# Adding the squares of a norm on GpSimd: two rows for TensorE to sum instead of eight

## The chip, the cores and the metric

The kernel runs on one core of a Trainium2 chip. Its metric is the device time of one execution in microseconds (us), the median over runs. Five engines have their own instruction queues and meet through semaphores: TensorE (PE; its weight loads are listed apart as PEld), VectorE (DVE), ScalarE (ACT), GpSimd (POOL) and SyncE (SP), which issues most of the DMAs.

## The reference, cut to what matters

One inference step of a small hybrid decoder: 512 prompt tokens and 8 sample tokens, so N = 520 columns, with D_MODEL = 1024. Layer 0 mixes with a gated linear recurrence (HGRN2), layer 1 with sparse attention (NSA) over a key/value side that is projected once between the layers. Each layer adds its mixer and a squared-ReLU MLP to the residual stream x, and every mixer, MLP, the key/value projection and the output reads a normed x:

```python
def rmsnorm(x, g):
    xf = x.astype(jnp.float32)
    y = xf * lax.rsqrt(jnp.mean(xf * xf, axis=-1, keepdims=True) + RMS_EPS)
    return (y * g.astype(jnp.float32)).astype(x.dtype)

def sq_relu_mlp(h, w_up, w_down):
    return jnp.square(jax.nn.relu(h @ w_up)) @ w_down

def trunk(x, S_init, make_ctx, attend):
    ...
        x = x + o
        x = x + sq_relu_mlp(rmsnorm(x, norm_mlp[l]), w_mlp_up[l], w_mlp_down[l])
    return rmsnorm(x, norm_final), ...
```

So the sum that a norm needs runs over all 1024 features of a token.

## The kernel before, in words

Everything is transposed: a feature is a partition, a token a column. x, h and the MLP's hidden layer big are held as rows of 128 features by 520 tokens; x and h have KD = 8 rows each. All data are 32-bit floats, and a 128x128 by 128x260 product is two passes of the array in the trace (a row of the trace counts passes, the code and the listings of the order count products).

A dense layer (`dense`, `chunk_products`, matmul at line 827, `in_half` at 866 and `out_rows` at 881 for the ones that are interleaved with the recurrence) goes chunk by chunk: 128 output features, all 520 tokens in two halves of 260. Two pairs of PSUM banks alternate, `pair(c)`; the engine that empties a pair counts up `chunk_taken`, on which PE waits before it uses the pair again. Weights come as slabs of 2 MB through two buffers, issued by SP (line 471) when PE has finished the slab before the last (`chunk_ready`). So the order of the work is set by hand: each engine has one program, in order, and waits on semaphores.

The norms are called mix0, mlp0, attn (which serves the key/value projection, the gate and the query projection), mlp1 and final. Five pieces make one:

- `residual` (DVE, line 1921) adds a chunk of the dense layer before to row k of x as soon as the chunk is there.
- `norm_act` (ACT) squares row k of x into row k of `squares` (line 1410, counts norm["sq"]), and multiplies rows of x by the norm's gain into the input of the dense layer that follows (`gained`, line 1401, counts norm["out"]). A gain in the list `early` is applied to row k right behind its square; one in `late` is applied to all eight rows when the squares are done, because the buffer is still read until then.
- `norm_sum` (PE) multiplies `squares` by a matrix of ones (line 816), which adds up over the partitions and over the eight rows and leaves the sum in every partition of PSUM banks 6 and 7 (counts norm["sum"]).
- ACT takes the root into rstd (line 1417), and DVE inverts it (`norm_dve`, line 1779).
- The dense layer that follows doesn't wait for rstd: it runs on the gained x, and 1/rms is multiplied into its result when DVE empties a chunk (line 1930 for the MLPs, 1783 for key/value and query). It waits for norm["out"] alone. Only the final norm needs rstd first (line 2262), since its rows are turned and stored.

Of the lists, mlp0 has its gain in `late` (h), attn has key/value's in `early` (h) and query's in `late` (h2 in big), mlp1 has its gain in `late` (h is the input of the dense layer before it), and final has none. POOL builds factors in the recurrence's loop, waits for attn's norm at line 680, and then serves the attention.

Of the kernel before, what the change touches and what calls it, by code (L numbers as in the profile page):

```python
# [16 lines left out]
ALU = mybir.AluOpType  # L17
# [40 lines left out]
def hybrid_step(nc, ins, outs):  # L58
# [4 lines left out]
    KD = D // P  # L63
# [23 lines left out]
    with ctx:  # L87
# [3 lines left out]
        def sem(name):  # L91
            return ctx.enter_context(nc.semaphore(name))
# [3 lines left out]
        h = sb("h", [P, KD, N])  # L96
# [12 lines left out]
        GAIN_MIX, GAIN_MLP, GAIN_KV, GAIN_FINAL, GAIN_O, LOGITS = 0, 16, 32, 40, 48, 56  # L109
# [142 lines left out]
        relu_done = sem("relu_done")  # L252
        relu_base = {"up0": 0, "up1": KF}

        norm = {k: sem("norm_" + k) for k in ("sq", "sum", "sqrt", "out")}
        turn_of = {name: n for n, name in enumerate(("mix0", "mlp0", "attn", "mlp1", "final"))}
        out_count = {"mix0": KD, "mlp0": 2 * KD, "kv": 3 * KD, "attn": 4 * KD, "mlp1": 5 * KD, "final": 6 * KD}
        squares = scratch[:, 0:KD * N].rearrange("p (k t) -> p k t", k=KD)
# [363 lines left out]
        def _(pool):  # L622
            ch = Chain(pool, pool_chain)
# [13 lines left out]
            for l in range(7):  # L637
                m = 64 >> l
# [13 lines left out]
            for i in range(heads):  # L652
# [7 lines left out]
                for l in range(7):  # L660
                    m = 64 >> l
# [14 lines left out]
                        nc.gpsimd.tensor_tensor(qd, q, EB, ALU.mult).then_inc(hg["qd"], 1)  # L676


            pool.wait_ge(norm["out"], out_count["attn"])
            pool.wait_ge(norm["sum"], turn_of["attn"] + 1)  # L680
            ch.add(nc.gpsimd.memset(diag, 0.0))  # L681
# [101 lines left out]
            for s in range(16 * B):  # L783
# [4 lines left out]
                    pool.wait_ge(sm["turned"], s - 3)  # L788
                regroup(cmp_slot[e // 8], P, e % 8 // 4, e % 4, RGs[s % 4]).then_inc(sm["rg"], 1)


        @block.tensor
        def _(pe):
# [5 lines left out]
            for k in range(KD):  # L799
                m = nc.tensor.transpose(ps[:, 6, B * k:B * k + B], xs_rows[:, P * k:P * k + P], ident[0:B, 0:B])  # L800
# [3 lines left out]
            for k in range(KD):  # L804
                if k >= 4:
                    pe.wait_ge(turn_taken, 2 + k - 3)
                for a in range(TT):
                    m = nc.tensor.transpose(ps[:, k % 4, P * a:P * a + P], x_rows[:, a, P * k:P * k + P], ident[:])
                m.then_inc(turned, 1)

            def norm_sum(name, sq):
                n = turn_of[name]
                for k in range(KD):
                    pe.wait_ge(norm["sq"], n * KD + k + 1)
                    for a in range(2):
                        m = nc.tensor.matmul(ps[:, 6 + a, 0:NH], ones[:], sq[:, k, NH * a:NH * a + NH],  # L816
                                             start=(k == 0), stop=(k == KD - 1))
                m.then_inc(norm["sum"], 1)
# [77 lines left out]
            for i in range(heads + 1):  # L896
# [13 lines left out]
                if live:  # L910
# [4 lines left out]
                    for c in range(TT):  # L915
                        m = nc.tensor.transpose(ps[:, 6, P * c:P * c + P], V[i % 2][:, P * c:P * c + P], ident[:])
                    m.then_inc(hg["vt"], 1)
                dense_half(i, 0)
                if prev:
# [4 lines left out]
                    for c in range(TT):  # L924
                        m = nc.tensor.matmul(ps[:, 7, P * c:P * c + P], vtok[(i - 1) % 2][:, P * c:P * c + P],
                                             AT[:, P * c:P * c + P], start=True, stop=(c == 0))
                        if c:
                            m = nc.tensor.matmul(ps[:, 7, P * c:P * c + P], St[:, c - 1, :],
                                                 qd[:, P * c:P * c + P], start=False, stop=True)
# [5 lines left out]
                if live:  # L935
# [4 lines left out]
                    for c in range(TT):  # L940
                        m = nc.tensor.matmul(ps[:, 4, P * c:P * c + P], Kb[:, P * c:P * c + P],
                                             Q[i % 2][:, P * c:P * c + P], start=True, stop=True)
# [3 lines left out]
                    for c in range(TT):  # L946
                        m = nc.tensor.transpose(ps[:, 6, P * c:P * c + P], kd[:, P * c:P * c + P], ident[:])
# [6 lines left out]
                if live:  # L954
                    level(1)
                    pe.wait_ge(hg["ktok"], i + 1)
                    for c in range(TT):
                        m = nc.tensor.matmul(ps[:, 6, P * c:P * c + P], ktok[:, P * c:P * c + P],
                                             vtok[i % 2][:, P * c:P * c + P], start=True, stop=True)
# [7 lines left out]
                if prev:  # L967
# [3 lines left out]
                    for b in range(B):  # L971
                        m = nc.tensor.matmul(ps[:, 6, b:b + 1], S0[(i - 1) % 2][:, b, :], Q[(i - 1) % 2][:, T + b:T + b + 1],
                                             start=True, stop=True)
# [44 lines left out]
            for u in range(3 * TT):  # L1018
# [3 lines left out]
                for c in range(4):  # L1022
                    m = nc.tensor.transpose(ps[:, u % 4, P * c:P * c + P], KVT[:, 4 * cg + c, P * a:P * a + P], ident[:])
                m.then_inc(kt_ready, 1)
            for c in range(12):
                m = nc.tensor.transpose(ps[0:B, 4 + c // 4, P * (c % 4):P * (c % 4) + P], KVT[:, c, T:N], ident[:])
# [27 lines left out]
            for i in range(2):  # L1054
                m = nc.tensor.transpose(ps[:, 4, 16 * i:16 * i + 16], pe_rows[0:16, i, :], ident[0:16, 0:16])
# [3 lines left out]
            for i in range(2):  # L1059
                for k in range(16):  # L1060
                    m = nc.tensor.matmul(ps[0:DK, 5, i:i + 1], W1[i][:, k % 8, k // 8, :], pe_cols[:, i, k:k + 1],
                                         start=(k == 0), stop=(k == 15))
# [6 lines left out]
            for u in range(9):  # L1069
# [5 lines left out]
                if u:  # L1075
                    v = u - 1
                    pe.wait_ge(pc[f"ev{v % 2}"], v // 2 + 1)
                    rows = TK[v % 2].rearrange("p (g s a) -> p g s a", g=G, a=2)
# [3 lines left out]
            for g in range(G):  # L1082
                m = nc.tensor.matmul(ps[0:NB_P, 5, DK * g:DK * g + DK], Hp[:, G + g, :], W2[1], start=True, stop=True)
# [252 lines left out]
            for p in range(2):  # L1336
                i = 10 + p
                pe.wait_ge(kv_in[kv_slot(i)], kv_count(i))
                for c in range(4):
                    for j in range(4):  # L1340
                        m = nc.tensor.matmul(ps[32 * j:32 * j + 32, 6, GD * p:GD * p + GD], PTw[:, c, 32 * j:32 * j + 32],
                                             kv_tile(i)[:, j, c, :], start=(c == 0), stop=(c == 3))
# [4 lines left out]
            for p in range(2):  # L1347
                for q in range(4):
# [4 lines left out]
                    for c in range(4):  # L1353
                        for j in range(4):
                            m = nc.tensor.matmul(ps[32 * j:32 * j + 32, bank_of(0), GD * p:GD * p + GD],
                                                 PTs[:, 4 * q + c, 32 * j:32 * j + 32], kv_tile(i)[:, j, c, :],
                                                 start=(q == 0 and c == 0), stop=(q == 3 and c == 3))
                    m.then_inc(sm["out"], 1)
            pe.wait_ge(sm["acc"], past["acc"] + 1)
            for pr in range(2):  # L1360
                m = nc.tensor.transpose(ps[:, 0, P * pr:P * pr + P], acc[:, P * pr:P * pr + P], ident[:])
# [13 lines left out]
            for u in range(2 * TT):  # L1375
# [5 lines left out]
                for c in range(4):  # L1381
                    m = nc.tensor.transpose(ps[:, u % 4, P * c:P * c + P], h[:, 4 * cg + c, P * a:P * a + P], ident[:])
                m.then_inc(yturned, 1)
            for c in range(KD):
                m = nc.tensor.transpose(ps[0:B, 4 + c // 4, P * (c % 4):P * (c % 4) + P], h[:, c, T:N], ident[:])
# [4 lines left out]
        def _(act):  # L1390
            ch = Chain(act, act_chain)
# [12 lines left out]
            def norm_act(name, sq, wait_row, early=(), late=()):  # L1404


                n = turn_of[name]
                for k in range(KD):
                    wait_row(k)
                    nc.scalar.activation(sq[:, k, :], x[:, k, :], ACT.Square).then_inc(norm["sq"], 1)  # L1410
                    for gain, out in early:
                        gained(gain, out, k)
                for gain, out in late:
                    for k in range(KD):
                        gained(gain, out, k)
                act.wait_ge(norm["sum"], n + 1)
                nc.scalar.activation(halves(rstd[:]), ps[:, 6:8, 0:NH], ACT.Sqrt, bias=eps[:], scale=1.0 / D)\
                    .then_inc(norm["sqrt"], 1)

            def added(name):  # L1420

                def wait_row(k):
                    c = chunk_base[name] + k
                    act.wait_ge(chunk_taken[c % 2], taken(c % 2, c + 1))
                return wait_row
# [102 lines left out]
                    gate_in(i + 1)  # L1528
            act.wait_ge(hg["r"], heads)

            norm_act("mlp0", squares, added("out"), late=[(GAIN_MLP, h)])

            def settle_chunks(eng, n):
                for p in range(2):
# [6 lines left out]
            for n in range(KD):  # L1541
                c = chunk_base["q"] + n
                act.wait_ge(chunk_taken[c % 2], taken(c % 2, c + 1))
                for a in range(2):
                    m = nc.scalar.activation(h[DK * (1 - a):DK * (1 - a) + DK, n, 0:T], QT[DK * a:DK * a + DK, n, 0:T], ACT.Copy)
# [751 lines left out]
```

## Time and profile before

| what | value |
|---|---|
| runs shown | 2308.98 us median of 3 (2304.52, 2308.98, 3209.32) |
| the profiled execution | 2305.89 us |
| its span, first to last instruction | 2303.9 us |
| PE matmul busy | 92% of the span |
| ACT busy / DVE busy / POOL busy | 18% / 27% / 13% |
| mean granted clock of TensorE | 0.952 of full speed |

The span is what the rows below are read against; 2.0 us of the execution lie around it. A shape 128x260 is partitions by columns. `xN` counts instructions of a group. In a granted clock 1.00 is 2.4 GHz and 0.50 is 1.2 GHz.

### The profile page before, as it was taken

The numbers are of one execution on the slowest core, as the hardware profiler recorded it, in microseconds if no ns is written. First come the engines' busy times: TensorE is split into PE (matmuls) and PEld (weight loads), VectorE is DVE, ScalarE is ACT, GpSimd is POOL, SyncE is SP. The second block draws the span as 40 slices with busy tenths as digits, with TensorE's granted clock in tenths as the row PEclk, the third lists the DMA queues.
The fourth block names the chain that finished last, engine by engine and source line by source line (L and its number), as shares of the span: only waits on it lengthen the run. The fifth ranks groups of instructions, "written<-read, shape, count | busy, mean of one in ns | idle before, by whom it ended". The sixth has DMA issues, their size and how long they took to land.

```text
span 2303.9 us, 28903 instructions
## 1 busy us (share of the span) xinstructions
PE 2114.3 (92%) x11468; PEld 1769.1 (77%) x11468; DVE 613.9 (27%) x1084; ACT 407.3 (18%) x839; POOL 294.5 (13%) x523
## 2 busy tenths in 40 slices
PE   6999998999999999999688888899846999999997
PEld 5888887888888888887565667688514888888886
DVE  2455556121110000102244453344410111110002
ACT  2344443110000000102133332233300100000000
POOL 2233234000000000000223333342000000000000
PEclk8999999999999999999589999999967999999999
DMA  4322321122222222233600004997786022222221
GB/s 129 78 63 66 93 66 58 46 74 73 73 73 73 73 73 73 73 113 129 148 1 1 1 1 105 216 188 185 230 255 213 1 73 73 73 73 73 73 73 37
DMA packets 216475, 206.87 MB, mean 90 GB/s; under 512 B 13857, under 2 KB 170642, under 8 KB 216242
## 3 DMA queue, kind: packets, MB, share of 16 engines
q1 hardware_dynamic: 203122, 193.39, 30.0%
q10 hardware_dynamic: 13248, 12.06, 1.6%
q8 instruction: 67, 1.10, 0.2%
q14 instruction: 38, 0.31, 0.1%
HBM read 195.38 MB, written 18.42 MB: 93 GB/s over the span
## 4 chain that ended last, share of the span: by engine, by line
PE 83%; SPq 4%; DVE 3%; DMA 2%; POOL 2%; issue 2%; ACTq 2%; ACT 1%; DVEq 0%; POOLq 0%
PE ps L827 49%; PE ps L866 10%; PE ps L1045 4%; PE ps L1121 4%; PE ps L1038 2%; PE ps L906 2%; PE ps L816 2%; PE ps L1139 2%; SPq L582 1%; POOL scratch L725 1%; DMA stream<-in_cache_nsa_kv 1%; PE ps L881 1%; SPq L343 1%; PE ps L1099 1%; ACTq L1670 1%
## 5 line engine op out<-in xcount | busy, mean ns | idle before, releaser
L827 PE MATMUL ps<-h,stream 128*128 128x260 f32 x2688 | 592.3, 384 | 1.7 <-DVE h L2253 1.7
L827 PEld LDWEIGHTS ps<-h,stream 128*128 128x128 f32 x2688 | 512.1, 191 | 81.4 <-DVE h L2253 2.1
L827 PE MATMUL ps<-big,stream 128*128 128x260 f32 (+1 forms) x2464 | 542.9, 383 | 4.8 <-DVE big L1933 4.0
L827 PEld LDWEIGHTS ps<-big,stream 128*128 128x128 f32 (+1 forms) x2464 | 466.9, 190 | 80.5 <-issue 5.1
L866 PE MATMUL ps<-h,stream 128*128 128x260 f32 x1024 | 237.0, 386 | 5.1 <-DVE h L1788 5.1
L866 PEld LDWEIGHTS ps<-h,stream 128*128 128x128 f32 x1024 | 191.7, 192 | 37.2 <-issue 10.0
L1410 ACT ACTIVATE scratch<-x 128x520 f32<-128x520 f32 x32 | 20.4, 637 | 1052.8 <-DVE x L1921 1052.8
L1921 DVE TENSOR_TENSOR x<-x,ps 128x520 f32 x32 | 22.3, 696 | 537.4 <-PE ps L827 521.7
L1930 DVE SCALAR_TENSOR_TENSOR scratch<-ps,rstd 128x520 f32<-128x520 f32 x64 | 44.8, 699 | 343.2 <-PE ps L827 343.2
L1121 PE MATMUL ps<-scratch,big 128*128 128x128 f32 x640 | 92.2, 297 | 44.1 <-POOL scratch L725 44.1
L1121 PEld LDWEIGHTS ps<-scratch,big 128*128 128x128 f32 x640 | 81.6, 204 | 53.5 <-issue 48.3
L1045 PE MATMUL ps<-big 128*128 128x256 f32 x384 | 99.7, 383 | 0.0
L1590 ACT ACTIVATE big<-ps,scratch 128x128 f32<-128x128 f32 (+3 forms) x128 | 66.3, 522 | 151.5 <-DVE scratch L2023 151.5
L2099 DVE COPY big<-ps 128x512 f32<-128x512 f32 x80 | 55.3, 691 | 109.1 <-PE ps L1038 76.9
L1835 DVE COPY_PREDICATED scratch<-scratch,ps 128x512 f32<-128x512 int32 x64 | 47.0, 734 | 121.7 <-PE ps L906 100.7
L702 POOL COPY scratch<-stream 128x512 f32<-128x512 f32 (+1 forms) x72 | 42.8, 613 | 254.7 <-DMA stream<-out 168.5
L1640 ACT ACTIVATE big<-ps 128x512 f32<-128x512 f32 x81 | 48.2, 597 | 135.3 <-PE ps L1038 93.1
L725 POOL TENSOR_SCALAR scratch<-ident,scratch 128x128 f32<-128x128 f32 x128 | 56.2, 449 | 124.3 <-DVE scratch L2029 124.3
L1045 PEld LDWEIGHTS ps<-big 128*128 128x128 f32 x384 | 66.0, 192 | 5.4 <-DVE big L2099 0.3
L681 POOL MEMSET scratch<- 128x128 f32 x1 | 0.2, 207 | 542.5 <-ACT big L1401 542.5
L906 PEld LDWEIGHTS ps<-scratch 128*128 128x128 f32 x448 | 59.8, 199 | 9.8 <-POOL scratch L670 5.2
L906 PE MATMUL ps<-scratch 128*128 128x128 f32 x448 | 62.7, 285 | 3.7 <-POOL scratch L670 3.7
(308 smaller groups left out, 2068.8 us busy)
## 6 DMA issues: line engine op xcount, KB each, us to landing
stream<-in_w_mlp_up SPq DMA_DIRECT2D x16, 2048.0 KB, 8.9
stream<-in_w_mlp_down SPq DMA_DIRECT2D x16, 2048.0 KB, 9.0
stream<-in_cache_nsa_kv SPq DMA_DIRECT2D x128, 256.0 KB, 6.1
stream<-in_cache_nsa_kv SPq DMA_DIRECT2D x164, 128.0 KB
stream<-in_w_hgrn_in SPq DMA_DIRECT2D x32, 512.0 KB, 6.7
stream<-in_cache_nsa_kv ACTq DMA_DIRECT2D x92, 128.0 KB
stream<-in_cache_win_kv SPq DMA_DIRECT2D x16, 512.0 KB
out<-in_cache_win_kv SPq DMA_DIRECT2D x8, 1022.0 KB
```

The source lines that it names most:

```text
L725: m = nc.gpsimd.tensor_scalar(Dg[u % 4][:, br, :], ident[:], wts[u % 4][:, br:br + 1], gtok[:, t, gate:gate + 1], ALU.mult, ALU.mult)
L816: m = nc.tensor.matmul(ps[:, 6 + a, 0:NH], ones[:], sq[:, k, NH * a:NH * a + NH], start=(k == 0), stop=(k == KD - 1))
L827: m = nc.tensor.matmul(pair(c)[0:n1, a, :], w[:, k, P * c_local:P * c_local + n1], rhs[:, k, NH * a:NH * a + NH], start=(k == 0), stop=(k ...
L866: m = nc.tensor.matmul(pair(c)[:, a, :], w[:, k, :], h[:, k, NH * a:NH * a + NH], start=(k == 0), stop=(k == KD - 1))
L906: m = nc.tensor.matmul(ps[:, 5 - l % 2, P * c:P * c + P], Lv[l % 2][:, P * c:P * c + P], Lv[l % 2][:, P * c:P * c + P], start=True, stop=True)
L1038: m = nc.tensor.transpose(ps[:, bank, P * g:P * g + n], src[0:n, g, :], ident[0:n, 0:n])
L1045: m = nc.tensor.matmul(ps[:, bank, 0:G * n // 2], W1[kv][:, kk, :, :].rearrange("p a n -> p (a n)"), columns(par), start=(rp == 0 and par ...
L1121: m = nc.tensor.matmul(ps[:, bank, P * i:P * i + P], Pb[(2 * n + a) % 4][:, br, P * s:P * s + P], Dg[(2 * n + a) % 4][:, br, :], start=Tru ...
L1590: m = nc.scalar.activation(Pb[u % 4][:, br, 0:w], ps[:, 2 * a + br, 0:w], ACT.Exp, bias=nmax[a][:, br:br + 1], accum_out=sums[u % 4][:, br ...
L1640: nc.scalar.activation(out, ps[:, TB[s % 3], :], ACT.Copy).then_inc(sm["ev0"], 1)
L1835: nc.vector.copy_predicated(AT.rearrange("p (c t) -> p c t", c=TT), masks[:, mask:mask + 1, :].to_broadcast([P, TT, P]).bitcast(I32), ps[: ...
L2099: nc.vector.tensor_copy(out, ps[:, TB[s % 3], :]).then_inc(sm["ev1"], 1)
```

## The change

In four of the five norms (all but mix0) POOL now adds rows 1 to 6 of `squares` into row 0, one after the other, each when its square is there, and counts norm["added"] when row 6 is in. PE multiplies the ones by two rows only: the total in row 0 and row 7, the last. And mlp0's gain moves from `late` to `early`.

```diff
-        norm = {k: sem("norm_" + k) for k in ("sq", "sum", "sqrt", "out")}
+        norm = {k: sem("norm_" + k) for k in ("sq", "added", "sum", "sqrt", "out")}
...
+            def squares_added(name):
+
+                n = turn_of[name]
+                total = squares[:, 0, :]
+                pool.wait_ge(norm["sq"], n * KD + 1)
+                for k in range(1, KD - 1):
+                    pool.wait_ge(norm["sq"], n * KD + k + 1)
+                    m = nc.gpsimd.tensor_tensor(total, total, squares[:, k, :], ALU.add)
+                    if k < KD - 2:
+                        ch.link(m)
+                m.then_inc(norm["added"], 1)
+
+            squares_added("mlp0")
+            squares_added("attn")
             pool.wait_ge(norm["out"], out_count["attn"])
...
+            squares_added("mlp1")
+            squares_added("final")
...
             def norm_sum(name, sq):
                 n = turn_of[name]
-                for k in range(KD):
-                    pe.wait_ge(norm["sq"], n * KD + k + 1)
+                rows = range(KD) if name == "mix0" else (0, KD - 1)
+                for k in rows:
+                    if name == "mix0":
+                        pe.wait_ge(norm["sq"], k + 1)
+                    elif k == 0:
+                        pe.wait_ge(norm["added"], n)
+                    else:
+                        pe.wait_ge(norm["sq"], n * KD + KD)
                     for a in range(2):
                         m = nc.tensor.matmul(ps[:, 6 + a, 0:NH], ones[:], sq[:, k, NH * a:NH * a + NH],
                                              start=(k == 0), stop=(k == KD - 1))
...
-            norm_act("mlp0", squares, added("out"), late=[(GAIN_MLP, h)])
+            norm_act("mlp0", squares, added("out"), early=[(GAIN_MLP, h)])
```

`squares_added("mlp1")` and `squares_added("final")` stand at the very end of POOL's program.

PE at mlp1, between the last chunk of the attention's output projection and the MLP's first chunk. Before (the sum is line 816, a dense layer 827):

```order
1850:1848 L816 MATMUL ps<-scratch,ones 128x260 [waits norm_sq]
1851:1849 L816 MATMUL ps<-scratch,ones 128x260
...
1864:1862 L816 MATMUL ps<-scratch,ones 128x260 [waits norm_sq]
1865:1863 L816 MATMUL ps<-scratch,ones 128x260
1866-1864 L850 UNCONDITIONAL_BRANCH [waits norm_out]
1867-1865 L850 ISA
1868-1866 L822 ISA [waits slab_in0]
1869-1867 L827 MATMUL ps<-h,stream 128x260 [waits chunk_taken1]
```

And now (the sum is line 839, a dense layer 850):

```order
1826:1824 L839 MATMUL ps<-scratch,ones 128x260 [waits norm_added]
1827:1825 L839 MATMUL ps<-scratch,ones 128x260
1828:1826 L839 MATMUL ps<-scratch,ones 128x260 [waits norm_sq]
1829:1827 L839 MATMUL ps<-scratch,ones 128x260
1830-1828 L873 UNCONDITIONAL_BRANCH [waits norm_out]
1831-1829 L873 ISA
1832-1830 L845 ISA [waits slab_in0]
1833-1831 L850 MATMUL ps<-h,stream 128x260 [waits chunk_taken1]
```

Sixteen products became four, in two steps with a wait each; the MLP's loop behind them still waits for norm["out"]. The same stands at mlp0, attn and final.

ACT at mlp0. Before, the eight squares (line 1410), then the eight gained rows (1401), then the root (1417):

```order
240:238 L1410 ACTIVATE scratch<-x 128x520 [waits chunk_taken0]
241:239 L1410 ACTIVATE scratch<-x 128x520 [waits chunk_taken1]
242-240 L1401 ACTIVATE h<-x,vec 128x520 x8
243-241 L1417 ACT_TABLE_LOAD
244-242 L1417 ACTIVATE rstd<-ps,eps 128x520 [waits norm_sum]
```

Now (1433, 1424, 1440):

```order
246:244 L1433 ACTIVATE scratch<-x 128x520 [waits chunk_taken0]
247-245 L1424 ACTIVATE h<-x,vec 128x520
248:246 L1433 ACTIVATE scratch<-x 128x520 [waits chunk_taken1]
249-247 L1424 ACTIVATE h<-x,vec 128x520
250-248 L1440 ACT_TABLE_LOAD
251-249 L1440 ACTIVATE rstd<-ps,eps 128x520 [waits norm_sum]
```

One gained row stands behind each square, and one instead of eight behind the last.

## Rows read from the trace of the kernel before

**Rows 1.** The page: the span, and the chain that ended last, by line.

```profile
span 2303.9 us, 28903 instructions
...
PE ps L827 49%; PE ps L866 10%; PE ps L1045 4%; PE ps L1121 4%; PE ps L1038 2%; PE ps L906 2%; PE ps L816 2%; PE ps L1139 2%; SPq L582 1%; POOL scratch L725 1%; DMA stream<-in_cache_nsa_kv 1%; PE ps L881 1%; SPq L343 1%; PE ps L1099 1%; ACTq L1670 1%
```

**Rows 2.** Timeline at mlp0: start, us, engine, line, instruction, [idle before <-releaser].

```profile
460.70 0.64 ACT L1410 ACTIVATE scratch<-x 128x520 f32<-128x520 f32 x1 [6.37 <-DVE x L1921]
...
466.67 7.18 PE L816 MATMUL ps<-scratch,ones 128*128 128x260 f32 x32
...
467.72 0.64 ACT L1410 ACTIVATE scratch<-x 128x520 f32<-128x520 f32 x1 [6.38 <-DVE x L1921]
468.27 5.04 ACT L1401 ACTIVATE h<-x,vec 128x520 f32<-128x520 f32 x8
...
473.69 26.53 PE L827 MATMUL ps<-h,stream 128*128 128x260 f32 x120
...
475.45 3.40 DVE L1779 RECIPROCAL rstd<-rstd 128x520 f32<-128x520 f32 x1 [7.76 <-ACT rstd L1417]
```

**Rows 3.** Timeline at attn.

```profile
927.65 0.64 ACT L1410 ACTIVATE scratch<-x 128x520 f32<-128x520 f32 x1 [26.82 <-DVE x L1921]
...
928.81 5.05 ACT L1401 ACTIVATE big<-x,vec 128x520 f32<-128x520 f32 x8
...
933.61 36.76 PE L827 MATMUL ps<-h,stream 128*128 128x260 f32 x167
```

**Rows 4.** Timeline at mlp1.

```profile
1819.68 7.18 PE L816 MATMUL ps<-scratch,ones 128*128 128x260 f32 x32
...
1820.74 0.64 ACT L1410 ACTIVATE scratch<-x 128x520 f32<-128x520 f32 x1 [6.39 <-DVE x L1921]
1821.28 5.04 ACT L1401 ACTIVATE h<-x,vec 128x520 f32<-128x520 f32 x8
...
1826.69 15.42 PEld L827 LDWEIGHTS ps<-h,stream 128*128 128x128 f32 x71 [0.23 <-issue]
```

**Rows 5.** Timeline at final.

```profile
2277.83 7.18 PE L816 MATMUL ps<-scratch,ones 128*128 128x260 f32 x32
...
2278.89 0.64 ACT L1410 ACTIVATE scratch<-x 128x520 f32<-128x520 f32 x1 [27.43 <-DVE x L1921]
2285.05 0.69 ACT L1417 ACTIVATE rstd<-ps,eps 128x520 f32<-128x520 f32 x1 [5.52 <-PE ps L816]
```

**Rows 6.** POOL's products of two 128x512 operands, lines 658 and 676: ns min/median/max.

```profile
L658 POOL TENSOR_TENSOR scratch<-scratch,stream x8: 1262/1265/1319, 72.7 to 373.3; 128x512 f32<-128x512 f32 x8
...
L676 POOL TENSOR_TENSOR scratch<-big,scratch x8: 1271/1726/1730, 86.2 to 381.6; 128x512 f32<-128x512 f32 x8
```

**Rows 7.** Timeline: PE behind five idle times, 0.79 to 5.11 us long.

```profile
1025.87 4.43 PE L827 MATMUL ps<-big,stream 128*128 128x260 f32 x19 [0.79 <-DMA stream<-in_w_nsa_q]
...
2053.30 16.92 PE L827 MATMUL ps<-big,stream 128*128 128x260 f32 x76 [1.92 <-DVE big L1933]
...
700.38 15.97 PE L827 MATMUL ps<-big,stream 128*128 128x260 f32 x64 [2.04 <-DVE big L1933]
...
421.16 17.62 PE L881 MATMUL ps<-big,stream 128*128 128x260 f32 x72 [3.83 <-DVE big L1902]
...
37.81 7.39 PE L866 MATMUL ps<-h,stream 128*128 128x260 f32 x23 [5.11 <-DVE h L1788]
```

**Rows 8.** Stretches after those idle times: length, busy time by engine, clock, DMA share, GB/s.

```profile
1026.00:1030.00 4.00, 4.00 (x19) 3.48 (x20) 0.00 (x0) 0.48 (x1) 0.00 (x0) 1.00 0.94 311
...
2054.00:2056.00 2.00, 2.00 (x11) 1.74 (x10) 0.00 (x0) 0.00 (x0) 0.00 (x0) 1.00 1.18 302
...
703.00:704.00 1.00, 1.00 (x3) 0.71 (x3) 0.00 (x0) 0.00 (x0) 0.00 (x0) 0.50 1.20 295
...
421.00:440.00 19.00, 18.84 (x79) 16.10 (x80) 2.89 (x5) 2.24 (x4) 0.00 (x0) 0.91 0.01 2
...
38.00:60.00 22.00, 22.00 (x92) 18.74 (x93) 5.91 (x10) 6.97 (x8) 0.00 (x0) 0.91 0.00 1
```

## The prediction

> **What bounds the kernel now.** I read the page first: the chain that ended last is PE over most of the span, the dense layers (lines 827 and 866) alone 59%, the norm's sum (816) 2% [rows 1]. So time comes off where PE's own work on that chain gets shorter, and only there. Then I read the timeline at each of the four norms. At mlp0 the sum is 32 passes in 7.18 us, started right behind the dense layer; the last pass takes 0.38 us (7.18 less 31 steps of 0.219). The square of row 7, the last thing that it needs, runs on ACT from 467.72 to 468.36, and PE goes on with rows that are long there, until the dense layer starts at 473.69 [rows 2]. So 5.3 us of the sum lie behind the last square, on the path. At attn and final it is the same [rows 3, 5]. At mlp1 there is something else: ACT's eight late gained rows run from 1821.28 to 1826.32, and the next weight load comes at 1826.69, after 0.23 us idle [rows 4]. PE's loop there waits for those rows; the sum lies just beside them. Last I read the clock after PE's idle times [rows 7, 8], since the change puts idle time where PE had work.
>
> **The change part by part.**
>
> *PE's sum.* 32 passes become 8: 24 × 0.219 = 5.26 us of PE work less in each of four norms, 21.0 us in all. That is the most the change can take off. What of it counts depends on what is late next. The total of rows 0 to 6 must be there first. Row 6's square ends at 461.34 [rows 2], and one POOL add follows. The trace has no 128x520 add on POOL; the nearest rows are 128x512 products of two operands, 1.26 us at least and 1.73 at most [rows 6], so 1.3 to 1.8 us for 520 columns. I take 1.8, as the adds are in place in the same buffer. The total is there by 463.2, and PE comes at 466.67: 3.4 us to spare. At attn and final rows come 28 us apart (idle times of 26.82 and 27.43 us before ACT's last square [rows 3, 5]), at mlp1 7 us apart [rows 4], so POOL is hidden everywhere. If a POOL add took over 5 us this cover would be gone; see the rivals.
>
> PE then makes the 4 passes of the total (until 467.71), idles until the square of row 7 is seen, and makes the other 4. From the square's end to PE I take 0.07 us: a release between engines costs at least 0.04 (the sum ends at 2285.01, the root starts at 2285.05 [rows 5]) and, with a loop's entry on PE, at most 0.37 (1826.32 to 1826.69 [rows 4]); there is no loop entry here, so near the lower end. A restart costs 0.1: behind the 0.79 us wait 19 passes took 4.43 us, which is 18 steps of 0.225 where 0.219 is usual [rows 7].
>
> - mlp0: 468.36 + 0.07 + 0.1 + 4 × 0.219 = 469.41 for the first dense pass, before 473.69: **−4.28 us**. It needs the gained rows too, see the next item.
> - attn: 928.29 + 0.07 + 0.1 + 0.88 = 929.34, before 933.61: **−4.27 us**. Key/value's gain is in the early list already.
> - final: the sum's end becomes 2279.53 + 0.07 + 0.1 + 0.66 + 0.38 = 2280.74, before 2285.01: **−4.27 us**. ACT's root, DVE's inverse, the eight outputs and the stores follow from it and move as one.
> - mlp1: **nothing**. The gained rows still end at 1826.32, the loop entry still takes 0.37 us, and the dense layer starts at 1826.69 as now.
>
> *mlp0's gain early.* Same eight instructions on ACT, 0.63 us each (5.04 / 8 [rows 2]). Rows 0 to 6 now hide in the 6.37 us that ACT idles before each square. Behind the last square stands one: 468.27 + 0.71 = 468.98, and with 0.37 for the loop entry PE could start at 469.35, just under the 469.41 above. Without this part mlp0 would be like mlp1 and gain nothing. h is free to be written: the layer before reads big. The root and inverse move up too. From the last gained row to the end of the inverse it is 5.54 us now (473.31 to 478.85), so rstd is there by 474.5, and DVE needs it when PE ends the first chunk, 7 us after 469.41. At attn the late rows for h2 still end at 933.86; 5.54 us at most behind them rstd is there, by 939.4, and the buffer that DVE empties with it is wanted by PE for the third chunk, at 929.34 + 14.0 = 943.4. No wait there.
>
> *New idle time and the clock.* Three norms' sums get one wait of 0.7 us (467.71 to 468.43). At mlp1 PE ends the sum at about 1822.6 (1821.38 + 0.07 + 0.1 + 0.66 + 0.38) and has nothing until 1826.7: 4.1 us. The trace shows what idle times do: behind 0.79 us the granted clock was 1.00 (2.4 GHz), behind 1.92 us 1.00, behind 2.04 us it went to 0.50 (1.2 GHz), and behind 3.83 and 5.11 us the stretches that follow had a mean of 0.91 [rows 7, 8]. 19 us at 0.91 are 1.7 us lost, 22 us at 0.91 are 2.0. So at mlp1 I take a loss of 1.7 us, by the row nearest in length (3.83 us), with bounds of 0 and 2.0; at the 0.7 us waits none, by the 0.79 us row, with 1.7 each as the bound at mlp0 and attn. At final the dense work is over. mlp1 is then the one place where the change costs: **+1.7 us**.
>
> A rule speaks against the change here: the Trainium skill, "TensorE: Matmul & The Clock Gate", section "A second HAM failure mode: psum-queue depth-cycling", says that short idle times between groups of matmuls can be enough to make the clock swing between its levels. By that rule the sum would be −7.7 us; the 0.79 us row, at full clock behind it, doesn't agree.
>
> *The rest.* POOL's 24 adds stand where POOL waits anyway; its next work after attn waits for the late rows that end at 933.86 as now. SP's slab loads hang on PE's chunks and move with them.
>
> Sum: −4.28 − 4.27 − 4.27 + 1.7 = −11.1 us. Against the profiled execution's 2305.89 us (2303.9 of span and 2.0 around it): **2294.8 us**. That execution lies 3.1 us under the shown median of 2308.98 and 1.4 over the lowest run.
>
> **The rivals.**
>
> - *The clock falls at the short waits too.* Then mlp0 and attn each lose 1.7 us of their 4.27: 2294.8 + 3.4 = 2298.2. For it: nearly equal idle times of 1.92 and 2.04 us went different ways, so length alone doesn't settle it. Against: 0.79 us of idle in the same kind of work kept 1.00. This is what the rule above would bring.
> - *The clock is kinder.* mlp1's wait doesn't lower it (2293.1), or the 2.04 us wait at 700, which the change shifts by 4 us, goes as its twin of 1.92 us did, for about as much again: 2291.4 with both. The twin could as well fall in its place, +1.7.
> - *The gain is given back.* mlp0's and attn's dense layers start early but wait for rstd or a buffer later, so that only final's 4.27 stay, less mlp1's 1.7: 2303.3. For it: rstd moves by nothing at attn. Against: the slack of 2 and 4 us worked out above.
> - *POOL becomes what PE waits for, and the kernel gets slower.* Place: mlp0 and mlp1, where rows come 7.0 us apart. Six adds follow on each other, so an add over 7.0 us makes a chain that starts at row 1's square, near 426.3, and the dense layer follows six adds and 8 passes (1.85 us) later. mlp0 breaks even at (473.69 − 1.85 − 426.3) / 6 = 7.6 us an add, mlp1 much the same; the whole kernel at 8.2, when the two have eaten the 8.5 us of attn and final less 1.7. At 10 us an add each of the two would lose some 14 us: about 2328. Against: the rows show 1.73 us at most [rows 6].
>
> **How the numbers follow.** Forecast 0.70, clock falls at short waits 0.12, kinder clock 0.10, given back 0.05, POOL 0.01, and 0.02 for what I don't see. The time is the forecast's, 2294.8. The range: down from 2294.8 to 2291.4 for the kinder clock, less 1.4 for a run like the lowest and 2 for my restart and release times, 2288; up to 2298.2 and 3.1 more for runs about the median, 2301.3, and 2 for the same doubts, 2303. "Given back" stays half outside, slower outside.
>
> 2%, about what a measurement of this kernel can tell from no change, is 46 us. The change removes 21.0 us of PE work at most, so faster by over 2% is 0.01; slower by over 2% needs POOL adds of over 12 us or something unseen, 0.01; the same 0.98.
>
> **What would show it.** The sum as two groups of 8 passes in all with 0.7 us between them, and the dense layer 1.1 us behind the last square at mlp0 and attn; the root at final 1.3 us behind it; at mlp1 an idle time of about 4 us that ends with the late rows, and a lower clock behind it; POOL adds under 2 us, the last ending well before PE reaches the total. I am wrong if PE waits for POOL, if the clock falls behind the short waits, or if DVE waits for rstd in the first chunks.

## The result, and the profile after

The changed kernel takes **2295.66 us** (median of 5 runs, 2294.29 to 2297.96) against 2309.15 us for the kernel before (5 runs, of which the one at 3209.32 us is left out of the ratio): a ratio of 0.9946, 95% interval 0.9930 to 0.9961. That is 12.5 us less by the ratio, clear of zero and far below 2%. 2294.8 was forecast, 11.1 us under the profiled execution of before; the profiled execution of the changed kernel takes 2295.66 us with a span of 2293.8, 10.2 us under it.

The line numbers have moved by 23: the sum is now line 839, a square 1433, a gained row 1424, the root 1440, the dense layer 850, POOL's add 686. The timeline of the changed kernel at mlp0, against [rows 2] (start, us, engine, line, instruction, idle before and who ended it):

```profile
457.79 0.64 ACT L1433 ACTIVATE scratch<-x 128x520 f32<-128x520 f32 x1 [5.75 <-DVE x L1944]
458.33 0.71 ACT L1424 ACTIVATE h<-x,vec 128x520 f32<-128x520 f32 x1
458.57 1.28 POOL L686 TENSOR_TENSOR scratch<-scratch 128x520 f32<-128x520 f32 x1 [5.72 <-ACT scratch L1433]
463.76 1.04 PE L839 MATMUL ps<-scratch,ones 128*128 128x260 f32 x4
...
464.81 0.64 ACT L1433 ACTIVATE scratch<-x 128x520 f32<-128x520 f32 x1 [5.76 <-DVE x L1944]
465.35 0.71 ACT L1424 ACTIVATE h<-x,vec 128x520 f32<-128x520 f32 x1
...
465.50 1.14 PE L839 MATMUL ps<-scratch,ones 128*128 128x260 f32 x4 [0.70 <-ACT scratch L1433]
...
466.48 18.82 PE L850 MATMUL ps<-h,stream 128*128 128x260 f32 x85
```

Row 6's square ends at 458.43, POOL's last add at 459.85, and PE comes for the total at 463.76, 3.9 us later. The last square ends at 465.45; PE is idle for 0.70 us, makes 4 passes and starts the dense layer at 466.48, 1.03 us behind the square where it was 5.33.

At attn (against [rows 3]) and final (against [rows 5]) the same picture:

```profile
920.41 0.64 ACT L1433 ACTIVATE scratch<-x 128x520 f32<-128x520 f32 x1 [26.82 <-DVE x L1944]
...
921.10 1.14 PE L839 MATMUL ps<-scratch,ones 128*128 128x260 f32 x4 [0.70 <-ACT scratch L1433]
921.57 5.04 ACT L1424 ACTIVATE big<-x,vec 128x520 f32<-128x520 f32 x8
...
922.08 20.11 PE L850 MATMUL ps<-h,stream 128*128 128x260 f32 x91
...
927.32 3.40 DVE L1802 RECIPROCAL rstd<-rstd 128x520 f32<-128x520 f32 x1 [6.95 <-ACT rstd L1440]
930.76 0.70 DVE L1806 TENSOR_TENSOR big<-ps,rstd 128x520 f32<-128x520 f32 x1
...
936.30 0.70 DVE L1806 TENSOR_TENSOR big<-ps,rstd 128x520 f32<-128x520 f32 x1 [4.85 <-PE ps L850]
```

```profile
2272.74 0.64 ACT L1433 ACTIVATE scratch<-x 128x520 f32<-128x520 f32 x1 [27.43 <-DVE x L1944]
...
2273.43 1.14 PE L839 MATMUL ps<-scratch,ones 128*128 128x260 f32 x4 [0.71 <-ACT scratch L1433]
2274.61 0.69 ACT L1440 ACTIVATE rstd<-ps,eps 128x520 f32<-128x520 f32 x1 [1.23 <-PE ps L839]
```

At attn rstd still comes late, since ACT's eight late rows stand ahead of the root; DVE empties the first chunk only when the inverse is done (930.72), but the second chunk waits for PE again (4.85 us). PE doesn't wait for rstd there; only at final does the path go through it.

At mlp1 (against [rows 4]) the last square ends at 1811.88 and the dense layer starts at 1817.16, 5.28 us later, where it was 5.32. In between PE is now idle:

```profile
1811.24 0.64 ACT L1433 ACTIVATE scratch<-x 128x520 f32<-128x520 f32 x1 [6.39 <-DVE x L1944]
1811.79 5.04 ACT L1424 ACTIVATE h<-x,vec 128x520 f32<-128x520 f32 x8
...
1811.93 1.14 PE L839 MATMUL ps<-scratch,ones 128*128 128x260 f32 x4 [0.70 <-ACT scratch L1433]
...
1817.16 28.03 PE L850 MATMUL ps<-h,stream 128*128 128x260 f32 x119 [4.09 <-ACT h L1424]
```

Stretches of the changed kernel (length, busy us by engine with counts, granted clock, DMA share, GB/s): behind the 4.09 us wait of mlp1, and around the 0.70 us waits of mlp0 and attn.

```profile
1817.00:1821.00 4.00, 3.84 (x10) 3.06 (x11) 2.04 (x1) 1.82 (x2) 0.00 (x0) 0.57 0.02 4
462.00:468.00 6.00, 5.30 (x24) 4.19 (x23) 0.70 (x1) 3.16 (x4) 0.00 (x0) 1.00 0.47 159
919.00:925.00 6.00, 5.30 (x25) 4.28 (x24) 0.70 (x1) 4.59 (x8) 0.00 (x0) 1.00 0.74 245
```

The clock falls behind the long wait (4.00 us at 0.57, 1.7 us lost) and stays at 1.00 through the short ones.

It also falls at a place that the change doesn't touch, behind the wait between the second MLP's two layers (a row of the timeline, then a stretch):

```profile
2045.47 14.88 PE L850 MATMUL ps<-big,stream 128*128 128x260 f32 x59 [1.93 <-DVE big L1956]
...
2046.00:2050.00 4.00, 4.00 (x12) 3.17 (x11) 0.00 (x0) 0.00 (x0) 0.00 (x0) 0.57 1.18 306
```

Where the 10.1 us between the two spans went, from landmarks in both timelines (S is the end of a norm's last square, D the first pass of the dense layer behind it; final's D is the root):

| stretch | before | after | difference |
|---|---|---|---|
| start to S of mlp0 | 468.36 | 465.45 | -2.91 |
| S to D at mlp0 | 5.33 | 1.03 | -4.30 |
| D at mlp0 to S of attn | 454.60 | 454.57 | -0.03 |
| S to D at attn | 5.32 | 1.03 | -4.29 |
| D at attn to S of mlp1 | 887.77 | 889.80 | +2.03 |
| S to D at mlp1 | 5.32 | 5.28 | -0.04 |
| D at mlp1 to S of final | 452.83 | 456.22 | +3.39 |
| S to root at final | 5.52 | 1.23 | -4.29 |
| root to the end | 18.85 | 19.19 | +0.34 |

The +3.39 is two half-clock stretches of 1.7 us: the one behind mlp1's wait, and one at 2046, behind a wait of 1.93 us that is there in the kernel before too, at 2053 (1.92 us), and left the clock alone that time [rows 7, 8]. The second may not be chance: over the profiles of all the kernels in this document, that wait lowered the clock in five of the seven that have the short sum at mlp1 and in none of the three that have the long one. Ten profiles are too few to tell, and no run here shows what decides it.

The -2.91 and the +2.03 lie where the change does nothing. The first is there before the first add: PE's row behind the 3.83 us wait starts at 418.35, where it was 421.16. Over the profiles the start to S of mlp0 took 465.1 to 468.4 us, with the change and without. The +2.03 lies in the attention over the cache: from attn's D to the last transposes it was 825.2 and 825.6 us in the two kernels without the adds, and 825.4 to 828.7 us in those with them, where attn's D is the same point.

### The profile page after: what moved, and what is told of

Read it like the earlier page. It is cut to its first block, busy times and chain, and to the rows that moved or that the text cites. A ratio compares the mean times of both kernels' runs of the same rounds, so it can differ in the third digit from the quotient of the medians.

```text
span 2293.8 us, 28759 instructions
## 1 busy us (share of the span) xinstructions
PE 2093.6 (91%) x11372; PEld 1751.5 (76%) x11372; DVE 613.3 (27%) x1084; ACT 407.4 (18%) x839; POOL 326.4 (14%) x547
## 4 chain that ended last, share of the span: by engine, by line
PE 84%; DVE 4%; SPq 3%; DMA 2%; POOL 2%; issue 2%; ACTq 2%; ACT 1%; DVEq 0%; POOLq 0%
PE ps L850 49%; PE ps L889 10%; PE ps L1068 5%; PE ps L1144 4%; PE ps L1061 2%; PE ps L929 2%; PE ps L1162 2%; DMA stream<-in_cache_nsa_kv 1%; POOL scratch L739 1%; SPq L582 1%; PE ps L904 1%; PE ps L1122 1%; SPq L343 1%; ACTq L1693 1%; DVE stream L2061 1%
## 5 line engine op out<-in xcount | busy, mean ns | idle before, releaser
L686 POOL TENSOR_TENSOR scratch<-scratch 128x520 f32<-128x520 f32 x24 | 30.9, 1287 | 1144.1 <-ACT scratch L1433 1144.1
```

## The experiments

Times are medians; ratios are to the kernel before on the same chip. All start from the changed kernel unless the text says otherwise.

**The adds alone: mlp0's gain late again.**

```diff
-            norm_act("mlp0", squares, added("out"), early=[(GAIN_MLP, h)])
+            norm_act("mlp0", squares, added("out"), late=[(GAIN_MLP, h)])
```

> The changed kernel with mlp0's gain back in the late list (the adds on GpSimd and the sums of two rows stay). Theory (the sum counts only where the gained rows are early): from the end of mlp0's last square to the first pass of the dense layer some 5.3 us as in the kernel before (1.03 in the changed kernel), with about 4.1 us of it idle and the granted clock at 0.50 behind it, as at mlp1; so 4.3 us and about 1.7 us more than the changed kernel, in all some 5 us under the kernel before: about 2301. Rival (the adds alone make the gain, the order of the gained rows is no matter): the same 1.0 us and about 2296.

2303.31 us (11 runs), ratio 0.9988 (0.9979 to 0.9997). Its timeline at mlp0:

```profile
467.48 0.64 ACT L1433 ACTIVATE scratch<-x 128x520 f32<-128x520 f32 x1 [6.38 <-DVE x L1944]
...
468.17 1.14 PE L839 MATMUL ps<-scratch,ones 128*128 128x260 f32 x4 [0.70 <-ACT scratch L1433]
...
473.40 6.84 PE L850 MATMUL ps<-h,stream 128*128 128x260 f32 x18 [4.09 <-ACT h L1424]
```

and the stretch behind it:

```profile
473.00:477.00 4.00, 3.60 (x8) 2.86 (x9) 1.80 (x1) 2.04 (x3) 0.00 (x0) 0.50 0.16 57
```

S to D is 5.28 us, the 4.09 us are idle, ended by ACT's gained rows, and the clock is at 0.50. mlp0 now looks like mlp1. The rival (the order doesn't matter) is out. Of the 5 us that should have stayed against the kernel before, about 2.8 did (interval 0.7 to 4.8): the half clock cost 2.7 us at mlp0 and 1.95 at mlp1, where 1.7 was expected at each, and in this profile it came behind the 1.92 us wait at 2055 as well, for 1.7 more (1024 passes in 226.38 us; 224.69 in the kernel before).

**The early gain alone**, in the kernel before.

```diff
-            norm_act("mlp0", squares, added("out"), late=[(GAIN_MLP, h)])
+            norm_act("mlp0", squares, added("out"), early=[(GAIN_MLP, h)])
```

> The kernel before with mlp0's gain in the early list and nothing else changed. Theory: PE's sum of eight rows still lies behind the last square, so from that square's end to the dense layer it is 5.1 to 5.3 us as before, and the time is that of the kernel before within 0.5 us; only the inverse of the root comes earlier, by up to 0.5 us after the sum's end, which nobody waits for. Rival (the gained rows alone held the dense layer): 4 us less.

2305.19 us (11 runs), ratio 0.9998 (0.9989 to 1.0007): no difference that the runs can tell (about 2 us either way), as the theory had it. S to D at mlp0 is 5.32 us, with PE in its sum:

```profile
464.33 7.18 PE L816 MATMUL ps<-scratch,ones 128*128 128x260 f32 x32
...
465.38 0.64 ACT L1410 ACTIVATE scratch<-x 128x520 f32<-128x520 f32 x1 [5.76 <-DVE x L1921]
...
471.34 8.93 PE L827 MATMUL ps<-h,stream 128*128 128x260 f32 x40
```

So at mlp0 neither part gains without the other: the sum and the gained rows end at the same time, and the later of them sets the start.

**mlp1's sum of eight rows again.** `squares_added("mlp1")` is left out, and PE sums all rows there.

```diff
-                rows = range(KD) if name == "mix0" else (0, KD - 1)
+                rows = range(KD) if name in ("mix0", "mlp1") else (0, KD - 1)
                 for k in rows:
-                    if name == "mix0":
-                        pe.wait_ge(norm["sq"], k + 1)
+                    if name in ("mix0", "mlp1"):
+                        pe.wait_ge(norm["sq"], n * KD + k + 1)
                     elif k == 0:
-                        pe.wait_ge(norm["added"], n)
+                        pe.wait_ge(norm["added"], {"mlp0": 1, "attn": 2, "final": 3}[name])
```

> The changed kernel, but mlp1's sum takes all eight rows on PE again, as before the change (three norms keep the adds). Theory (the short sum at mlp1 brings nothing and leaves PE idle for 4.1 us, whereupon the clock falls): the dense layer of mlp1 starts 5.3 us behind the last square as in both kernels, PE is not idle there, the granted clock stays 1.00 behind it, and the stretch from there to the last square of final is about 1.7 us shorter than in the changed kernel; about 2294 in all. Rival (the clock falls there for another cause, or the loss is none): the stretch is as long as in the changed kernel, 2295.7.

2291.64 us (5 runs), ratio 0.9937 (0.9923 to 0.9950), 2 us under the changed kernel by the ratios; their intervals overlap, so the trace has to decide. At mlp1:

```profile
1809.41 7.18 PE L838 MATMUL ps<-scratch,ones 128*128 128x260 f32 x32
...
1810.46 0.64 ACT L1432 ACTIVATE scratch<-x 128x520 f32<-128x520 f32 x1 [6.39 <-DVE x L1943]
1811.01 5.04 ACT L1423 ACTIVATE h<-x,vec 128x520 f32<-128x520 f32 x8
...
1816.42 13.81 PE L849 MATMUL ps<-h,stream 128*128 128x260 f32 x62
```

with the clock behind it:

```profile
1817.00:1821.00 4.00, 4.00 (x20) 3.48 (x19) 2.81 (x1) 1.05 (x2) 0.00 (x0) 1.00 0.02 4
```

S to D is 5.32 us with 24 passes more, and the clock stays at 1.00 where the changed kernel had 0.57. From S of mlp1 to S of final it is 458.12 us, against 461.50 in the changed kernel and 458.15 in the kernel before; 1.7 us of that is this place, the rest the stretch at 2046, whose counterpart kept its clock here (1024 passes in 224.69 us, against 226.38 in the changed kernel).

**mlp1's gain early too.** h is read until the last chunk of the layer before, so the gained rows go where the squares were, and the squares into rows 12 to 19 of big, which are free then.

```diff
-            norm_act("mlp1", squares, added("nsa_out"), late=[(GAIN_MLP + KD, h)])
+            norm_act("mlp1", squares_in, added("nsa_out"), early=[(GAIN_MLP + KD, squares)])
...
-            norm_sum("mlp1", squares)
+            norm_sum("mlp1", squares_in)
             pe.wait_ge(norm["out"], out_count["mlp1"])
-            dense("up1", 8, h, KD, 512, turns=4)
+            dense("up1", 8, squares, KD, 512, turns=4)
...
-            squares_added("mlp1")
+            squares_added("mlp1", squares_in)
```

> The changed kernel with mlp1's gained rows early too: they go into the buffer of the squares, and mlp1's squares into free rows of big, since h is still read. Theory: from the last square's end to mlp1's dense layer 1.0 to 1.1 us where it is 5.3 now (4.3 less), one idle time of 0.7 us, and no lower clock behind it (1.7 less): about 6 us under the changed kernel, 2289.7. Rival (something else, a slab or the chunk buffers, holds the dense layer at mlp1): under 2 us less.

2287.99 us (5 runs), ratio 0.9922 (0.9908 to 0.9935): 18 us under the kernel before, 5.5 under the changed one by the ratios, where 6 was expected.

```profile
1812.06 0.64 ACT L1433 ACTIVATE big<-x 128x520 f32<-128x520 f32 x1 [5.78 <-DVE x L1944]
...
1812.75 1.14 PE L839 MATMUL ps<-big,ones 128*128 128x260 f32 x4 [0.70 <-ACT big L1433]
...
1813.73 16.63 PE L850 MATMUL ps<-scratch,stream 128*128 128x260 f32 x75
```

S to D is 1.03 us, and from 1817 to 1821 the clock is 1.00. So mlp1 could have had what the others got; what held it was the late list.

**POOL's adds three times, six times and eight times as many.** Ahead of each add stand two, five or seven more, into unused columns:

```diff
+                    for r in range(2):   # 5, 7
+                        ch.link(nc.gpsimd.tensor_tensor(scratch[:, 7200:7200 + N], squares[:, k, :], squares[:, k, :], ALU.add))
                     m = nc.gpsimd.tensor_tensor(total, total, squares[:, k, :], ALU.add)
```

> The changed kernel with two more adds of the same size, into unused columns, ahead of each of GpSimd's six adds, so that a row takes some 3 x 1.3 = 4 us there. Theory (POOL's adds are hidden: in the changed kernel the last one is done 3.7 us before PE reaches the total at mlp0): the total is there about 1 us before PE, the distance from the last square to the dense layer stays 1.0 us at mlp0 and attn, 5.3 at mlp1, and the time is the changed kernel's, 2295.7, within 2 us. Rival (POOL's work costs others something, by memory shared with DVE and ACT, or its releases are late): several us more.

2297.3 us (6 runs), ratio 0.9967 (0.9955 to 0.9979). By the medians that is 1.6 us over the changed kernel, by the ratios 4.8, where 2 were allowed; the intervals overlap, so the trace has to decide. At mlp0:

```profile
467.02 1.14 PE L841 MATMUL ps<-scratch,ones 128*128 128x260 f32 x4 [0.70 <-ACT scratch L1435]
...
468.00 8.30 PE L852 MATMUL ps<-h,stream 128*128 128x260 f32 x37
```

S to D is 1.03 us at mlp0 and attn and 5.28 at mlp1, as in the changed kernel. Its span is 1.6 us longer, and 1.5 of that is there before the first add (GpSimd's first add starts at 425.04, 423.51 in the changed kernel). So POOL's work is hidden and costs its neighbours nothing that the trace shows.

> The same with five more adds ahead of each, so that a row takes some 8 us on GpSimd, more than the 7.0 us between two rows at mlp0 and mlp1. Theory (six adds in a chain from row 1's square on, then 8 passes): at mlp0 the chain ends near 423.5 + 6 x 8.1 = 472.1 and the dense layer starts near 474 where it is 466.5 now, 7.5 us later, with a lower clock behind it (1.7); at mlp1 some 3.3 us later than now; nothing at attn and final, where rows come 28 us apart. In all 12 us over the changed kernel: about 2308, that is, where the kernel before stands. Rival (only the last add counts, since the others hide between rows): 8 us behind row 6's square at mlp0, mlp1, attn and final alike, some 3 us each at most, below 2300.

2296.61 us (4 runs), ratio 0.9960 (0.9944 to 0.9975): not 2308. The size of the experiment was wrong, not yet the theory. The extra adds read one row twice and took 1.05 us each, not 1.3:

```profile
459.86 5.57 POOL L687 TENSOR_TENSOR scratch<-scratch 128x520 f32<-128x520 f32 x5
465.51 1.28 POOL L688 TENSOR_TENSOR scratch<-scratch 128x520 f32<-128x520 f32 x1
...
466.85 2.02 PE L841 MATMUL ps<-scratch,ones 128*128 128x260 f32 x8 [1.67 <-POOL scratch L688]
...
468.70 7.62 PE L852 MATMUL ps<-h,stream 128*128 128x260 f32 x34
```

A row took 7.0 us, just the distance between rows. PE did wait for POOL at mlp0, and S to D became 2.00 us, 0.97 more; at mlp1 it waited as long, but the late gained rows came later still (5.28 us). That is all. The number was corrected and the edge crossed:

> The changed kernel with seven more adds ahead of each of GpSimd's six. In pool_x6 an extra add, which reads one row twice, took 1.11 us from start to start, so a row took 7.0 us there and the chain did not form; here a row takes 7 x 1.11 + 1.45 = 9.2 us. Theory (six rows in a chain from row 1's square on, then 8 passes): at mlp0 the dense layer starts 6 x 9.2 + 2.0 = 57.4 us behind row 1's square, where it is 43 us now, so 14 us later; at mlp1 52.5 - 5.3 + ... the same chain against a dense layer that starts 47.4 us behind row 1's square now, so 10 us later; with a lower clock behind mlp0's wait 1.7 more; nothing at attn and final. Some 26 us over the changed kernel: about 2322, slower than the kernel before by 13 to 16 us. Rival (only one row's work counts, 9.2 us behind row 6's square): 3.2 us later at mlp0, nothing at mlp1, about 2300.

2321.88 us (4 runs), ratio 1.0066 (1.0049 to 1.0082): 26 us over the changed kernel by the medians (28 by the ratios), slower than the kernel before. At mlp0, whose last square ends at 467.32:

```profile
471.74 7.83 POOL L687 TENSOR_TENSOR scratch<-scratch 128x520 f32<-128x520 f32 x7
479.65 1.28 POOL L688 TENSOR_TENSOR scratch<-scratch 128x520 f32<-128x520 f32 x1
...
480.98 3.84 PE L841 MATMUL ps<-scratch,ones 128*128 128x260 f32 x8 [15.19 <-POOL scratch L688]
...
484.61 5.71 PE L852 MATMUL ps<-h,stream 128*128 128x260 f32 x25
```

POOL takes 9.3 us a row, and its six rows form a chain from row 1's square on (425.38, where its first add starts, to 480.93). S to D is 17.29 us at mlp0 (16.3 more than in the changed kernel) and 17.30 at mlp1 (12.0 more); 14 plus 1.7 and 10 were expected. The total agrees better than its parts: this profile kept its clock at both of the 2 us waits between up and down layers, 3.4 us less than in the changed kernel's. After 15 us of idle even the 8 passes run at the lower clock (3.84 us for 2.02). The rival of the prediction is real, and its point is near the one worked out there: 7.6 us a row for mlp0 and 8.2 for the whole kernel were worked out; 7.0 changes next to nothing, 9.3 makes the kernel slower than before.

**The sum behind the first chunk**, on top of mlp1's early gain. The dense layer starts at once, its first chunk waiting for each gained row, and the sum follows that chunk at mlp0, attn and mlp1 (the up layers are written out instead of looped).

```diff
-            norm_sum("mlp0", squares)
-            pe.wait_ge(norm["out"], out_count["mlp0"])
-            dense("up0", 8, h, KD, 512, turns=4)
+            dense("up0", 8, h, KD, 512, row_there=lambda k: pe.wait_ge(norm["out"], KD + k + 1), between=lambda: norm_sum("mlp0", squares))
...
                     for k in range(k_rows):
+                        if row_there and a == 0:
+                            row_there(k)
...
+                            if between and s == n == 0:
+                                between()
```

> The kernel mlp1_early with the sum moved behind the first chunk of the dense layer at mlp0, attn and mlp1 (the first chunk waits for each gained row by itself; the MLP's up layers are written out instead of looped, since their first chunk differs). Theory: PE has no idle time at those norms any more; the dense layer starts 2.7 us earlier, the sum's 8 passes (1.75 us) come 7 us later, 1.0 us saved at each of three norms: 2285 against 2288. The inverse of the root then ends some 13 us behind the dense layer's start, before the second chunk ends at 15.8, so nobody waits for it. Rival 1 (DVE gets rstd too late and PE waits for a chunk buffer): PE idle before the third chunk, nothing saved. Rival 2 (the longer program without loops costs instruction loading): stretches of the up layers longer than in mlp1_early.

2285.17 us (5 runs), ratio 0.9910 (0.9896 to 0.9923), the fastest of all and 21 us under the kernel before by the ratio. At mlp0:

```profile
465.61 7.18 PE L852 MATMUL ps<-h,stream 128*128 128x260 f32 x32
...
472.62 1.92 PE L839 MATMUL ps<-scratch,ones 128*128 128x260 f32 x8
474.37 15.94 PE L852 MATMUL ps<-h,stream 128*128 128x260 f32 x72
...
475.40 3.40 DVE L1801 RECIPROCAL rstd<-rstd 128x520 f32<-128x520 f32 x1 [8.77 <-ACT rstd L1439]
479.03 0.70 DVE L1952 SCALAR_TENSOR_TENSOR scratch<-ps,rstd 128x520 f32<-128x520 f32 x1 [0.23 <-DVE rstd L1801]
```

PE has no idle time; from the end of the layer before to the second chunk it is 8.76 us, where the changed kernel needs 9.73 (463.76 to 466.48, and a chunk of 7.01). DVE now waits for rstd, as rival 1 said, but PE doesn't wait for DVE. Three times 0.97 is 2.9, and 2.8 were measured between the medians; the two kernels' intervals overlap, and this profile also kept its clock at both of the 2 us waits between up and down layers, so the distances in the trace carry the reading more than the times. Rival 2 (the longer program) fell: behind the first chunk the up layer's 992 passes take 217.58 us, as in mlp1_early (224.62 for 1024, of which the first chunk is 7.01).

## Why the prediction was right

*The sum at mlp0, attn and final.* −4.28, −4.27 and −4.27 were worked out; −4.30, −4.29 and −4.29 are measured. The release from ACT to PE was taken as 0.07 us and is 0.05 (465.45 to 465.50), the restart as 0.1 and is 0.10 (0.98 us from the first pass of row 7 to the dense layer, less 4 × 0.219). A POOL add takes 1.28 us; 1.8 was taken, where the trace of before had rows from 1.26 to 1.73 [rows 6], and since it is hidden the difference shows nowhere.

*mlp1 gains nothing and loses the clock.* The dense layer starts with the gained rows as said, PE is idle for 4.09 us (4.1 said), and the clock costs 1.7 us (1.7 said). Two runs turn the reading round: with eight rows back on PE the clock's loss goes and the late start stays; with the rows early both go. That the size came out at 1.7 is in part luck: behind the same wait of 4.09 us the fall cost 1.6 us in the kernel with three times the adds, and 1.95 and 2.7 with the adds alone.

*The early gain is needed at mlp0.* Shown from both sides: alone it brings nothing, and without it the adds bring nothing there and cost the clock.

*The rivals.* The clock at the short waits: of the 0.7 us waits ahead of a dense layer, the two of the changed kernel and the three of mlp1_early kept the clock at 1.00; that rival fell. "Given back" fell: rstd is late at attn and PE doesn't notice. One of the prediction's signs of being wrong did appear there, though: DVE waits for rstd in the first chunk. The second chunk is emptied from 936.30 on and a chunk takes 7.0 us, so the first stood ready near 929.3 and was emptied from 930.76 on, 1.5 us later. The prediction's own times (the first chunk at 929.34 + 7.0, rstd by 939.4) already allowed such a wait; what mattered is that PE wants the buffer only for the third chunk. So the sign was too strict, not the sum. POOL as the bound was shown to be what it would be, at 7.0 and 9.3 us a row where the change has 1.28.

*What the sum left out.* 1.1 us between its −11.2 (as measured) and the −10.1 of the spans: a half-clock stretch of 1.7 us at 2046, and −2.91, +2.03 and +0.34 in places that the change doesn't touch. The range had these as its allowance for runs. That they belong to the change in some way isn't excluded by single profiles; for the clock at 2046 the profiles taken together point that way without showing it (none of three with the long sum at mlp1, five of seven with the short one). That the forecast lies within 1 us of the median is partly luck: these places nearly cancel (+1.2), and 11.1 taken from the shown median instead of the profiled execution would have given 2297.9.

## What to carry to other kernels

Before work is taken from the engine that sets the time, look for what else releases its next piece: here two things, the sum and the gained rows, ended together, and only removing both moved the start. Where just the sum went, PE was idle for 4.09 us in the place of the work, the start didn't move, and the clock that fell behind the idle time cost 1.6 to 2.7 us. GpSimd's adds, made row by row, cost nothing at 3.5 us a row, 1 us at one norm at 7.0 us, which is just the distance between rows, and 12 to 16 us at each of two norms at 9.3 us, where the delay of every row adds to the next one's.

## What the runs showed of the hardware

- A GpSimd add of two 128x520 rows, in place, took 1.28 us; with one row as both operands and other columns as its output it took 1.05. Which of the two differences makes it shorter, no run separates.
- TensorE's clock stayed at its upper level through idle times of 0.70 us in the norms' sums, and fell behind 4.09 us each time it was seen (mlp1 of the changed kernel; mlp0 and mlp1 with the adds alone; mlp1 with three times the adds). Around 2 us it went both ways at the same place in the program: between the first MLP's two layers it fell behind 2.01 to 2.04 us in eight of the ten kernels profiled here, and kept its level behind 2.02 and 2.03 us in the other two; between the second MLP's layers it fell behind 1.92 or 1.93 us in five of the ten and kept its level behind the same wait in the other five. A fall behind these waits cost 1.7 us of the 1024 passes that follow (226.38 us for 224.69), more than half of what separates some of these kernels.
